# Moving the decays of a chunked scan on VectorE, and joining the scan's block to the projection behind it

## Chip, cores, metric

One core of a Trainium2 chip. The metric is the device time of one execution in microseconds; three timed runs of the kernel before gave 2123.28, 2125.17 and 2125.89 (median 2125.17).

## What is computed

Two transformer blocks in a row, on 1024 tokens of width 1024, all in float32: first one with a linear recurrence, attention and an expert layer, then one with a selective state space scan beside a long convolution, an output projection with layer norm, and a gate with another layer norm. The change touches the second block's scan and its output projection. Cut to these (the names are the reference's):

```python
# ssd_chunked: 8 chunks of 128 tokens, 2 groups of 8 heads of width 64, state 128
xdt = xh * dt
a_cs = cumsum(dt * a)                                   # inside each chunk
ldec = exp(where(causal, a_cs[l] - a_cs[s], -inf))
cb = einsum('clgn,csgn->cgls', cc, bc)
y_diag = einsum('cgjls,csgjp->clgjp', cb * ldec, xdt)
states = einsum('clgn,cgjl,clgjp->cgjpn', bc, exp(a_cs[-1] - a_cs), xdt)
h = h * chunk_decay + states                            # from chunk to chunk
y_off = einsum('clgn,cgjpn,cgjl->clgjp', cc, h_before, exp(a_cs))
y = y_diag + y_off + d_skip * xh
y_ssm = group_rms_norm(y * silu(z)) * ssm_norm_g
out = concat([y_ssm, y_conf]) @ w_out + b_out           # 2048 x 1024
h = layer_norm(ALPHA * h + out, ln1_g, ln1_b)
```

`h * chunk_decay` is the decay that the change moves; `... @ w_out` is the projection that it joins to the scan.

## The kernel before

The program is a row of blocks. In a block each engine has its own list of instructions in an order written out by hand, and semaphores order the engines among each other; a block ends for all engines together. Two blocks concern the change.

**The scan's block** (its vector part ends with the scan). The scan runs over 16 steps i = 2c + g: chunk c, head group g. For each step:

- ScalarE: `decays(i)` waits for the cumulated sums, takes eight Relus (L2656), the chunk's decay factor (L2661) and an Exp over 128x1024 (L2664). At the head of a chunk `read_turned(c)` (L2670) copies the turned B matrix out of PSUM, behind `decays` of the even step and ahead of `decays` of the odd one. `conf_high_part` (L2674) is work for the projection.
- GpSimd: one multiply of 128x1024 (L2515), the Exp's result times `cb`. It waits for `cb_ready` of the chunk and for `decay_ready` of the step.
- TensorE: at the end of each odd step `chunk(c + 1)` (L2539 to L2544: eight turns of x, two of B, two products) for the next chunk is issued ahead of that odd step's own `outputs`. `outputs(i)` makes the state's part (L2565), turns the carried part (L2576) and adds the product inside the chunk (L2582). `carried(i + 1)` (L2553) multiplies the state, after `update(i - 1)`.
- VectorE: `carried(i)` (L2853) scales what TensorE's `carried(i)` gave; `evac_y(i - 1)` (L2829, four instructions) takes y out of PSUM; `update(i - 1)` decays the state (L2866, 128x512, all in SBUF) and adds the chunk's part from PSUM (L2867); `chunk_cb` (L2845, odd steps) masks the next `cb`, after `read_turned`; `inputs(i + 1)` (L2819, two instructions) scales the turned x. `chunk(c)` on TensorE waits for `inputs(2c - 1)`, which VectorE issues in the even step 2c - 2.

The state has two halves, one for each head group; `update(i)` touches the half of its own step.

**The projection's block.** `product(s, t, ...)` (L3071) multiplies token tile t with weight unit s in 24 matmuls of 512 columns: for each of eight slices k, high by high, high by low and low by high. The units are split on the chip: ScalarE rounds (`unit_high_part`, L3138) and the rest `ring - high` is taken by VectorE for unit 0 (`first_low`, L3198) and by GpSimd for units 1 to 5 (L3060). The first product of unit 0 waits for the low part slice by slice. `conf_low_part(t)` (L3202) splits the other operand. Then y is gated by z (`gate_y`, L3208; z is loaded by SP at L3025), its squares are summed (`square_sum`, L3213, and `square_sums` on TensorE, L3089), and the residual is loaded and added up from the products (L3253, L3257). The products rotate over seven banks of PSUM, so the eighth product waits for the first addition (`res_part`).

Of the kernel before, what the change touches and what calls it, by code (L numbers as in the profile page):

```python
# [7 lines left out]
F32 = mybir.dt.float32  # L8
F32R = mybir.dt.float32r
U32 = mybir.dt.uint32  # L10
ALU = mybir.AluOpType
# [3 lines left out]
P = 128  # L15
# [37 lines left out]
def program(nc, A, one_hot, out):  # L53
# [55 lines left out]
    with ctx:  # L109
# [2354 lines left out]
        nc.clear_and_free_semaphores(middle_sems)  # L2464
        with nc.Block() as block:
# [33 lines left out]

            @block.gpsimd  # L2500
            def _(pool):
# [7 lines left out]
                for i in range(STEPS):  # L2509
# [5 lines left out]
                    nc.gpsimd.tensor_tensor(by_head, by_head, over_heads, ALU.mult).then_inc(m_ready, 1)  # L2515

            @block.tensor
            def _(pe):
# [107 lines left out]
                for i in range(STEPS):  # L2626
                    if i % 2 and i + 1 < STEPS:
                        chunk(i // 2 + 1)
                    outputs(i)
                    if 2 <= i + 1 < STEPS:  # L2630
                        carried(i + 1)

# [123 lines left out]

            @block.vector
            def _(dve):
# [184 lines left out]
                for i in range(STEPS):  # L2943
# [14 lines left out]


        z_sb = tiles(0, KD)  # L2960
        y_high, y_low = rounded("y_high", 16, [P, KD, S]), rounded("y_low", 24, [P, KD, S])
        z_in = [sem(f"z_in{g}") for g in range(2)]
        gated_y, ysq_ready, ysum_ready, ysum_mm, yroot_ready = (sem(n) for n in (
            "gated_y", "ysq_ready", "ysum_ready", "ysum_mm", "yroot_ready"))
        y_high_ready, y_low_ready, y_scaled = sem("y_high_ready"), sem("y_low_ready"), sem("y_scaled")

        y_rs = rsm[:, 0:2 * NT]

        res = tiles(0, NT)
        h1T_high, h1T_low = rounded("h1T_high", 16, [P, KD, S]), rounded("h1T_low", 24, [P, KD, S])  # L2970
        unit_high = [rounded("unit_high", 34, [P, KD, HALF])[:], ring_low[:, (U_OUT2 + 2) % NU]]
        b_out, ln1_g, ln1_b = tiles(32), tiles(33), tiles(32)

        ple_at = [tiles(8, 12, HALF)[:, (NT * n + t) % 12] for n in range(2) for t in range(NT)]

        bn2 = router_w[:].rearrange("p k e -> p (k e)")[:, 0:12 * NT].rearrange("p (t s) -> p t s", t=NT)
        ln2_g, ln2_b = tiles(14), tiles(15)
        gate_sb = [tiles(32), tiles(33)]  # L2980
        res_in = [sem(f"res_in{j}") for j in range(2)]
        rows_in, tail_in = sem("rows_in"), sem("tail_in")
        ple_in = [sem(f"ple_in{j}") for j in range(3)]
        res_scaled, ln1_b_in = sem("res_scaled"), sem("ln1_b_in")
        unit_high_ready, unit_low_ready = sem("unit_high_ready"), sem("unit_low_ready")
        first_low_ready = sem("first_low_ready")
        out2_mm, res_part = sem("out2_mm"), sem("res_part")
        var1, root1, h1_ready, h1_tr = sem("var1"), sem("root1"), sem("h1_ready"), sem("h1_tr")
        h1T_high_ready, h1T_low_ready = sem("h1T_high_ready"), sem("h1T_low_ready")
        gate_mm, gate_ready, ple_read = (sem(n) for n in ("gate_mm", "gate_ready", "ple_read"))  # L2990

        GATE_LAG = 2
# [341 lines left out]
```

## Time and profile before

| | us |
|---|---|
| median of three runs | 2125.17 |
| profiled execution | 2123.88 |
| its span | 2122.2 |
| TensorE matmul, busy | 2038.4 (96%) |
| VectorE, busy | 1672.5 (79%) |
| ScalarE, busy | 1081.6 (51%) |
| GpSimd, busy | 237.5 (11%) |

The span runs from the first to the last instruction of the profiled execution; 1.7 us of that execution lie outside it. The scan takes the span's stretch from about 1753 to 1831 and the projection begins at 1833.8. Times of single instructions are given as start and duration from the span's start. Busy shares over the span don't tell what ends a stage: in the scan all of the engines wait for one another.

### The profile page before, as it was taken

The numbers are of one execution on the slowest core, as the hardware profiler recorded it, in microseconds if no ns is written. First come the engines' busy times: TensorE is split into PE (matmuls) and PEld (weight loads), VectorE is DVE, ScalarE is ACT, GpSimd is POOL, SyncE is SP. The second block draws the span as 40 slices with busy tenths as digits, with TensorE's granted clock in tenths as the row PEclk, the third lists the DMA queues.
The fourth block names the chain that finished last, engine by engine and source line by source line (L and its number), as shares of the span: only waits on it lengthen the run. The fifth ranks groups of instructions, "written<-read, shape, count | busy, mean of one in ns | idle before, by whom it ended". The sixth has DMA issues, their size and how long they took to land. (4 is left out here: it accounts for less than half of the span.)

```text
span 2122.2 us, 25232 instructions
## 1 busy us (share of the span) xinstructions
PE 2038.4 (96%) x9940; PEld 1588.7 (75%) x9940; DVE 1672.5 (79%) x1726; ACT 1081.6 (51%) x1267; POOL 237.5 (11%) x172
## 2 busy tenths in 40 slices
PE   6999999999988999999999989999999998899998
PEld 4767766777736888888888657888888875688876
DVE  5575448875587999999999769999999978955776
ACT  4388418883236777777777542112232168523134
POOL 0200100000000111111110230000000014233040
PEclk9999999999999999999999999999999999999999
DMA  7311332104399999999999631112122245333121
GB/s 296 111 40 40 126 118 75 41 10 102 160 355 346 371 402 393 394 399 390 403 391 398 205 145 43 60 61 79 40 90 99 100 141 197 149 129 119 40 80 60
DMA packets 131495, 381.95 MB, mean 180 GB/s; under 512 B 9735, under 2 KB 22567, under 8 KB 131400
## 3 DMA queue, kind: packets, MB, share of 16 engines
q1 hardware_dynamic: 117640, 341.02, 42.3%
q0 software_dynamic: 7536, 22.70, 4.4%
q10 hardware_dynamic: 6224, 16.93, 2.0%
q8 instruction: 64, 1.05, 0.2%
q14 instruction: 31, 0.25, 0.0%
HBM read 337.49 MB, written 43.07 MB: 179 GB/s over the span
## 5 line engine op out<-in xcount | busy, mean ns | idle before, releaser
L2765 DVE SCALAR_TENSOR_TENSOR arena<-arena,vecs 128x1023 f32<-128x1023 f32 (+14 forms) x240 | 304.3, 1268 | 7.1
L2292 DVE TENSOR_TENSOR w_low<-W,w_high 128x2048 fp32r<-128x2048 f32 x96 | 216.9, 2286 | 33.2 <-ACT w_high L2189 33.2
L2292 DVE TENSOR_TENSOR w_low<-arena,w_high 128x2048 fp32r<-128x2048 f32 x96 | 218.4, 2289 | 19.4 <-ACT w_high L2189 19.4
L2005 PE MATMUL Q<-hT_high,w_high 128*128 128x512 f32 (+1 forms) x736 | 230.3, 392 | 2.6 <-DVE hT_low L2275 1.9
L2005 PE MATMUL Q<-hT_low,w_high 128*128 128x512 f32 (+1 forms) x720 | 225.3, 391 | 0.0
L2189 ACT ACTIVATE w_high<-arena 128x2048 fp32r<-128x2048 f32 x96 | 184.2, 1920 | 73.4 <-PE Q L2080 73.4
L2005 PE MATMUL Q<-hT_high,ring_low 128*128 128x512 f32 x704 | 220.3, 390 | 0.0
L2189 ACT ACTIVATE w_high<-W 128x2048 fp32r<-128x2048 f32 x96 | 184.0, 1919 | 65.9 <-PE Q L2080 63.7
L2018 ACT ACTIVATE w_high<-W 128x1024 fp32r<-128x1024 f32 x44 | 46.6, 1058 | 251.8 <-PE Q L2005 243.0
L2005 PEld LDWEIGHTS Q<-hT_high,w_high 128*128 128x128 f32 (+1 forms) x736 | 135.5, 184 | 35.3 <-DVE hT_low L2275 2.1
L2080 PE MATMUL Q<-w_high,x_high 128*128 128x512 f32 x512 | 160.5, 395 | 1.0 <-DVE x_low L2300 1.0
L2080 PE MATMUL Q<-w_low,x_high 128*128 128x512 f32 x512 | 158.6, 391 | 0.0
L2080 PE MATMUL Q<-w_high,x_low 128*128 128x512 f32 x512 | 158.5, 391 | 0.0
L2005 PEld LDWEIGHTS Q<-hT_low,w_high 128*128 128x128 f32 (+1 forms) x720 | 134.2, 186 | 29.8
L2005 PEld LDWEIGHTS Q<-hT_high,ring_low 128*128 128x128 f32 x704 | 132.7, 188 | 27.7
L2080 PEld LDWEIGHTS Q<-w_low,x_high 128*128 128x128 f32 x512 | 96.8, 189 | 20.4
L2080 PEld LDWEIGHTS Q<-w_high,x_low 128*128 128x128 f32 x512 | 96.7, 189 | 20.3
L2080 PEld LDWEIGHTS Q<-w_high,x_high 128*128 128x128 f32 x512 | 95.7, 190 | 20.1 <-DVE x_low L2300 1.2
L582 PE MATMUL Q<-h_high,in_high 128*128 128x512 f32 x254 | 101.1, 398 | 0.0
L583 PE MATMUL Q<-h_high,ring_low 128*128 128x512 f32 x254 | 99.6, 392 | 0.0
L584 PE MATMUL Q<-h_low,in_high 128*128 128x512 f32 x254 | 99.4, 391 | 0.0
L2428 POOL DMA_INDIRECT tokens_acc<-arena,idx x16 | 50.4, 3150 | 343.7 <-DVE arena L2335 330.1
(504 smaller groups left out, 4138.5 us busy)
## 6 DMA issues: line engine op xcount, KB each, us to landing
arena<-in_w_dram SPq DMA_DIRECT2D x48, 2048.0 KB, 12.4
W<-in_w_dram SPq DMA_DIRECT2D x48, 2048.0 KB, 13.5
W<-in_w_mod_dram SPq DMA_DIRECT2D x12, 2048.0 KB, 8.7
W<-in_w_in_dram SPq DMA_DIRECT2D x12, 2048.0 KB, 8.4
W<-in_w_out_dram SPq DMA_DIRECT2D x6, 2048.0 KB, 9.9
spill<-arena ACTq DMA_DIRECT2D x24, 512.0 KB, 2.7
W<-in_w_in_dram SPq DMA_DIRECT2D x8, 1024.0 KB, 8.7
arena<-spill SPq DMA_DIRECT2D x3, 2048.0 KB, 12.6
```

The costliest lines, as they stand in the source:

```text
L582: nc.tensor.matmul(bank, w_high, h_high, start=first, stop=False)
L583: nc.tensor.matmul(bank, w_low, h_high, start=False, stop=False)
L584: return nc.tensor.matmul(bank, w_high, h_low, start=False, stop=last)
L2005: ins = nc.tensor.matmul(Q[rows, 2 * pair_of(n) + half, :], w[:, k], x[:, k, HALF * half:HALF * half + HALF], start=k == 0 and w is high a ...
L2018: nc.scalar.activation(high, src, ACT.Copy).then_inc(split_high, 1)
L2080: ins = nc.tensor.matmul(Q[:, bank + n, :], x[:, kx], w[:, k, HALF * n:HALF * n + HALF], start=kx == 0 and x is high and w is wh, stop=kx ...
L2189: nc.scalar.activation(split_of(r, j)[0][:], chunk_src(r, j), ACT.Copy).then_inc(high_ready, 1)
L2292: nc.vector.tensor_tensor(wl[:], chunk_src(r, j), wh[:].bitcast(F32), ALU.subtract).then_inc(low_v, 1)
L2428: nc.gpsimd.indirect_dma_start(out=tokens_acc, out_offset=bass.IndirectOffsetOnAxis(ap=idx[:, e:e + 1], axis=0), in_=y_e, in_offset=None, ...
L2765: ins = nc.vector.scalar_tensor_tensor(conf[:, i, j:], u[:, 0:S - j], w, conf[:, i, j:], ALU.mult, ALU.add)
```

## The change

Three edits, and one that follows from them. (1) The decay leaves `update`. A new `fade(i)` makes it, and both decays of a chunk are issued in the even step i: `fade(i - 1)` ahead of `update(i - 1)`, and `fade(i)` behind it, ahead of `inputs(i + 1)`. Chunks 1 to 6 have decays, as before. (2) The projection's block is no block of its own any more: each engine's list follows its list of the scan, and on VectorE and SP waits for the scan's last `outputs` stand where the block's end stood. (3) Unit 0 is split while the scan ends: ScalarE rounds its slices behind its last `conf_high_part`, with waits (`FREED_BY`) for the scan's last reads of the memory that the rounded slices take, and GpSimd takes the rest of the slices behind its last multiply; VectorE's `first_low` is gone.

```diff
+        FREED_BY = {0: (chunk_mm, NT), 3: (from_mm, STEPS - 3), 5: (from_mm, STEPS - 2), 6: (turned_ready, NT)}
...
             @block.sync
...
+                sync.wait_ge(stage_out[1], 16 * (len(staged) // 2))
+                sync.wait_ge(y_mm, STEPS)
+                for g in range(2):
+                    sync.dma_start(z_sb[:, 4 * g:4 * g + 4], spill[20 + 4 * g:24 + 4 * g].rearrange("m p n -> p m n"))\
+                        .then_inc(z_in[g], 16)
...
             @block.gpsimd
...
+                for s in range(6):
...
-                for s in range(1, 6):
...
+                        if t == 0:
+                            pe.wait_ge(unit_low_ready, KD * s + k + 1)
...
-                            pe.wait_ge(*((unit_low_ready, KD * (s - 1) + k + 1) if s else (first_low_ready, k + 1)))
...
+                    for k in range(KD):
+                        if s == 0 and k in FREED_BY:
+                            act.wait_ge(*FREED_BY[k])
+                        nc.scalar.activation(unit_high[s % 2][:, k], ring[slot][:, k], ACT.Copy)\
+                            .then_inc(unit_high_ready, 1)
...
             @block.vector
...
+                def fade(i):
+
+                    c, g = divmod(i, 2)
+                    if 1 <= c < NT - 1:
+                        dve.wait_ge(from_mm, i - 1)
+                        dve.wait_ge(factor_ready, i + 1)
+                        s3 = state[:, HALF * g:HALF * g + HALF].rearrange("p (h n) -> p h n", h=HPG)
+                        v_link(nc.vector.tensor_tensor(s3, s3, decay_of(i).broadcast_to((P, HPG, DK)), ALU.mult))
+
                 def update(i):
...
                         if c:
-                            dve.wait_ge(factor_ready, i + 1)
-                            s3 = sg.rearrange("p (h n) -> p h n", h=HPG)
-                            v_link(nc.vector.tensor_tensor(s3, s3, decay_of(i).broadcast_to((P, HPG, DK)), ALU.mult))
                             ins = nc.vector.tensor_tensor(sg, sg, Q[:, STATE_BANKS[i % 2], :], ALU.add)
...
                         evac_y(i - 1)
+                        if i % 2 == 0:
+                            fade(i - 1)
                         update(i - 1)
+                        if i % 2 == 0:
+                            fade(i)
...
                 conf_low_part(0)
                 evac_y(STEPS - 1)
...
-                for k in range(4):
-                    first_low(k)
                 conf_low_part(1)
-                for k in range(4, KD):
-                    first_low(k)
                 conf_low_part(2)
+                dve.wait_ge(y_out, STEPS)
                 for b in range(4):
                     gate_y(b)
```

The rest of the diff carries the projection's lists over unchanged.

## Rows read from the trace of the kernel before

**Rows 1.** Chain that ended last, by time: start us, us, engine, tile, line.

```profile
1832.98 0.70 DVE ring_low L3198
1833.82 34.56 PE Q L3071 x144
1872.05 55.93 PE Q L3071 x240
```

**Rows 2.** Windows: stretch, us, busy PE PEld DVE ACT POOL, PEclk, DMA, GB/s.

```profile
1771.82:1782.59 10.77, 8.74 (x62) 5.38 (x62) 10.01 (x20) 9.83 (x26) 4.82 (x3) 1.00 0.33 119
1782.59:1794.74 12.15, 10.40 (x62) 6.88 (x62) 9.72 (x20) 8.17 (x22) 4.74 (x2) 0.86 0.27 91
1805.51:1816.29 10.78, 8.75 (x63) 5.39 (x63) 10.02 (x20) 8.18 (x22) 4.69 (x2) 1.00 0.07 25
1830.86:1833.82 2.96, 0.00 (x0) 0.03 (x1) 1.96 (x6) 1.50 (x3) 0.00 (x0) 0.50 0.23 19
1833.82:1841.02 7.20, 7.20 (x25) 5.79 (x25) 6.41 (x10) 2.77 (x6) 0.00 (x0) 0.75 0.98 373
```

**Rows 3.** Timeline of VectorE, one chunk: start us, us, line, op, tiles, [idle].

```profile
1807.00 0.69 DVE L2866 TENSOR_TENSOR arena<-arena,small 128x512 f32<-128x512 f32 x1
1808.44 0.42 DVE L2845 TENSOR_TENSOR W<-Q,tri 128x256 f32<-128x256 f32 x1
1810.68 0.69 DVE L2853 TENSOR_TENSOR W<-Q,W 128x512 f32<-128x512 f32 x1 [0.62 <-PE Q L2553]
1812.32 1.86 DVE L2866 TENSOR_TENSOR arena<-arena,small 128x512 f32<-128x512 f32 x1
1814.94 1.29 DVE L2819 TENSOR_TENSOR arena<-Q,keep 128x512 f32<-128x512 f32 x2
```

**Rows 4.** Timeline of TensorE, same chunk: chunk and the even step's carried.

```profile
1805.51 1.09 PE L2539 MATMUL Q<-ident,arena 128*128 128x128 f32 x8 [0.20 <-DVE W L2819]
1814.96 1.12 PE L2553 MATMUL Q<-arena 128*128 128x512 f32 x2 [1.83 <-DVE arena L2867]
```

**Rows 5.** Timelines of ScalarE and GpSimd, the same chunk.

```profile
1807.31 0.39 ACT L2670 ACTIVATE W<-Q 128x256 f32<-128x256 f32 x1 [2.59 <-PE Q L2544]
1810.06 1.06 ACT L2664 ACTIVATE arena<-arena 128x1024 f32<-128x1024 f32 x1
1811.27 2.37 POOL L2515 TENSOR_TENSOR arena<-arena,W 128x1024 f32<-128x1024 f32 x1
```

**Rows 6.** Timelines of TensorE, VectorE and GpSimd, the chunk from 1762.28.

```profile
1762.28 1.04 PE L2539 MATMUL Q<-ident,arena 128*128 128x128 f32 x8
1760.67 1.29 DVE L2819 TENSOR_TENSOR W<-Q,keep 128x512 f32<-128x512 f32 x2
1769.04 0.68 DVE L2866 TENSOR_TENSOR arena<-arena,small 128x512 f32<-128x512 f32 x1
1769.24 2.70 POOL L2515 TENSOR_TENSOR W<-W 128x1024 f32<-128x1024 f32 x1 [0.56 <-ACT W L2664]
```

**Rows 7.** Timelines of several engines, from the scan's last chunk on.

```profile
1819.72 4.69 POOL L2515 TENSOR_TENSOR W<-W 128x1024 f32<-128x1024 f32 x2 [6.08 <-DVE W L2845]
1854.64 16.88 POOL L3060 TENSOR_TENSOR ring_low<-W,ring_low 128x512 fp32r<-128x512 f32 x8 [30.23 <-ACT ring_low L3138]
1942.03 10.04 POOL L3060 TENSOR_TENSOR ring_low<-W,ring_low 128x512 fp32r<-128x512 f32 x8 [21.30 <-ACT ring_low L3138]
1832.32 4.27 ACT L3138 ACTIVATE unit_high<-W 128x512 fp32r<-128x512 f32 x8 [9.49 <-PEq L2465]
1832.30 0.92 SPq L3025 DMA_DIRECT2D arena<-spill  x2
1840.95 4.63 DVE L3208 TENSOR_TENSOR arena<-arena 128x1024 f32<-128x1024 f32 x4 [0.79 <-DMA arena<-spill]
1877.63 0.69 DVE L3257 TENSOR_TENSOR arena<-arena,Q 128x512 f32<-128x512 f32 x1
1878.86 0.39 PE L3071 MATMUL Q<-unit_high,conf_high 128*128 128x512 f32 x1
```

More of the change, by code:

```diff
@@ L2631, in _, with product @@
                         carried(i + 1)
+                def product(s, t, bank, high, low, first=0, end=KD):
+                    w_high, w_low = unit_high[s % 2], ring_low[:, home_of(U_OUT2 + s)]
+                    for k in range(first, end):
+                        if t == 0:
+                            pe.wait_ge(unit_low_ready, KD * s + k + 1)
+                        for x, w in ((high, w_high), (high, w_low), (low, w_high)):
+                            ins = nc.tensor.matmul(Q[:, bank, :], x[:, k, tile_cols(t)], w[:, k],
+                                                   start=k == first and x is high and w is w_high,
+                                                   stop=k == end - 1 and x is low)
+                    return ins
@@ new lines, in turn_h1, with square_sums @@
+                def turn_h1(t):
+                    pe.wait_ge(h1_ready, t + 1)
+                    if t >= 2:
+                        pe.wait_ge(h1T_low_ready, t - 1)
+                    for k in range(KD):
+                        ins = nc.tensor.transpose(Q[:, 2 * (t % 2) + k // 4, P * (k % 4):P * (k % 4) + P],
+                                                  res[:, t, P * k:P * k + P], ident[:])
+                    ins.then_inc(h1_tr, 1)
+                def square_sums():
+                    pe.wait_ge(ysum_ready, 2)
+                    for g in range(2):
+                        for t in range(NT):
+                            ins = nc.tensor.matmul(Q[:, 7, NT * g + t:NT * g + t + 1], z_sb[:, 4 * g + 3, tile_cols(t)],
+                                                   ones[:, 0:1], start=True, stop=True)
+                    ins.then_inc(ysum_mm, 1)
@@ new lines, in _ @@
+                for s in range(2):
+                    for t in range(NT):
+                        i = NT * s + t
+                        if s == 0:
+                            pe.wait_ge(conf_low_ready, t + 1)
+                        if i in Y_BANKS:
+                            pe.wait_ge(y_out, STEPS - 2 + Y_BANKS.index(i) + 1)
+                        if i >= CONF_BANKS:
+                            pe.wait_ge(res_part, i - CONF_BANKS + 1)
+                        product(s, t, i % CONF_BANKS, conf_high, conf_low).then_inc(out2_mm, 1)
+                        if i == 5:
+                            square_sums()
@@ new lines, in _ @@
+                for i, (s, t) in enumerate(y_order):
+                    if s == 2:
+                        pe.wait_ge(y_low_ready, t + 1)
+                    for g in range(2):
+                        j = 2 * i + g
+                        pe.wait_ge(res_part, LEAVE if j < 4 else LEAVE + j - 3)
+                        product(s, t, 4 + j % 4, y_high, y_low, 4 * g, 4 * g + 4).then_inc(out2_mm, 1)
+                    if s == 3 and t in TURNS:
+                        turn_h1(TURNS[t])
+                for i, (n, t) in enumerate(g_order):
+                    if i < 4:
+                        pe.wait_ge(res_part, PARTS - 3 + i)
+                    else:
+                        pe.wait_ge(gate_ready, i - 3)
+                    if n == 0:
+                        pe.wait_ge(h1T_low_ready, t + 1)
+                    product(4 + n, t, 4 + i % 4, h1T_high, h1T_low).then_inc(gate_mm, 1)
+                    if i < len(LATE):
+                        turn_h1(LATE[i])
@@ L2969, in program @@
[L2969 to L2988, printed above, removed]
```

313 lines of the change are left out of this document (124 added, 189 removed).

## The prediction

> **What bounds the kernel now.** I read the chain of waits first, from its end. From 1833.82 on it is TensorE almost alone: the chain enters the output projection through one ScalarE rounding and one VectorE subtraction of the first weight unit and then stays on L3071 [rows 1]. So what lies ahead of 1833.82 moves the end of the kernel one for one, unless something behind it is late in its turn. The table by stage comes second: a chunk of the scan lasts 10.77 us from one start of `chunk` on TensorE to the next, 12.15 in the one with the clock at half speed for a part, and between the scan's last matmul and the first one of the projection TensorE does nothing for 2.96 us [rows 2]. Third, one chunk on each engine. I count from the start of `chunk` on TensorE, 1805.51; that start waited for VectorE's `inputs` [rows 4].
>
> The chunk is a ring of two halves. TensorE runs `chunk`, the odd step's `outputs` and `carried` without a pause; VectorE waits 0.62 us for that `carried` and goes on at 1810.68, 5.17 in [rows 3]. Then VectorE works alone: `carried`, `evac_y`, a decay, an add, `inputs`, and the next `chunk` may start. In this half the decay (L2866) takes 1.86 us instead of 0.69. It began at 1812.32 and ended at 1814.18; GpSimd's second multiply ran from 1811.27 to 1813.64 [rows 3, 5]. The decay ended 0.54 after it, and where GpSimd is idle it takes 0.69: it stood behind GpSimd. The other decay, at 1807.00, lies in the first half, where VectorE has 0.62 us over [rows 3].
>
> **Both decays in the even step.** No instruction is added or removed; six decays change place (i = 2, 4, ... 12), from the half where VectorE has time into the half where everybody waits for it. Each costs 0.72 us there: a decay and an add took 1.44 from 1807.00 to `chunk_cb` at 1808.44 [rows 3], and the add is as long as the decay. What could pay for it is GpSimd: without the decay, `chunk_cb` comes earlier, GpSimd may start its two multiplies earlier, and the blocked decay is released earlier. `chunk_cb` also needs ScalarE's `read_turned`, which ended at 1807.70, so it moves from 1808.44 to some 1807.8, by 0.6 [rows 3, 5]. The first multiply follows. But the second one also needs ScalarE's Exp of the same step, 1810.06 to 1811.12, and it started at 1811.27, 0.15 later: it can hardly start sooner [rows 5]. ScalarE's work hangs on `read_turned`, so on the start of the chunk, and doesn't move in the ring. So the first decay still ends at 1814.18, the add follows, the second decay adds its 0.72, and the ring grows by 0.70 (0.02 given back, bounds 0.1 if the second multiply followed `chunk_cb` in full, and 0.72). Four chunks run in this state, from 1771.82 to 1816.29: +2.8 us.
>
> The first two chunks are different, since ScalarE is the late one there. At i = 2 the decay pushes `inputs` from 1760.67 to 1761.39, it ends near 1762.7, and the `chunk` that began at 1762.28 begins 0.47 later [rows 6]. The next even step is the dear one. Its first decay ran at 1769.04, 0.20 ahead of GpSimd's multiply at 1769.24, which had to wait for it (2.70 us against 2.37) [rows 5, 6]. 0.47 later it would come at 1769.51 and finds GpSimd at work until 1769.24 + 2.37 = 1771.61. It ends at 1772.17; then the add (0.72), the second decay (0.72), `inputs` with its 1.35 to the next `chunk` (1814.94 to 1816.29) [rows 2, 3]: 1774.99 instead of 1771.82, +3.17. Were it early enough to slip in, the second decay would be the blocked one, and +2.2 would be left. The last chunk has no second decay and costs nothing. Scan: 3.17 + 4 x 0.70 = +6.0 us, bounds 2.5 and 6.0, and I take the upper one, since the Exp is the nearest row.
>
> That holds one slow chunk, as before had one: 12.15 against 10.77 us, 1.38, when the granted clock fell to the lower of its levels after TensorE had stood still for 1.8 us before a `carried` (as at 1814.96) [rows 2, 4]. After the change the same pause is followed by a second one, of 0.9 us ahead of `chunk` instead of 0.2. So a fall is at least as likely in each chunk: none gives -1.4, two +1.4, three +2.8.
>
> **One block, first unit split at the scan's end.** ScalarE's eight roundings (L3138) and the subtractions move behind the scan's last multiply, and VectorE's eight subtractions L3198 (0.70 us each, [rows 1]) go to GpSimd, beside the scan's last steps. In before's own times, as if the scan hadn't moved: GpSimd is through with the scan at 1819.72 + 4.69 = 1824.41 [rows 7]. Its eight subtractions take 10.04 us when VectorE is at other things and 16.88 when VectorE subtracts all the while, 1.25 and 2.11 each [rows 7]. Beside VectorE's last decay and three `conf_low` parts I put down 0.55 + 8 x 1.25 + 3 x 0.86 = 13.1, so the last part is there at 1837.5; the ends are 1834.5 and 1841.3. ScalarE stood idle for 9.49 us there [rows 7], and its roundings wait at most for the scan's last `carried`, so they aren't late.
>
> The Trainium skill, "GPSIMD Engine Reference", section 4.1 Engine selection, says that GpSimd is about two times slower than VectorE on elementwise work with two inputs, which speaks against this move. The rows give 1.25 against 0.70, 1.8 times [rows 1, 7]; by the rule (1.40 each, an estimate) the last part would come 1.2 us later, TensorE would gain 1.6 instead of the 1.8 below, and the sum would be +4.4 instead of +4.2.
>
> TensorE then goes from the scan straight into the first product, at 1830.86 instead of 1833.82. Before, that product took 7.20 us, with the clock at half speed for its first part [rows 2]; the same from 1830.86 ends at 1838.1, and GpSimd's last part allows 1838.2. Against 1841.02 that is 2.8 us. But the gain isn't kept. The eighth product, at 1878.86, must not overwrite its bank before VectorE has added the first product to the residual, which before was done at 1877.63 + 0.69 = 1878.32 [rows 7]. VectorE gets there through the loads of z (issued at 1832.30, waited for until 1840.95), the gating, the square sums and the loads of the residual [rows 7]. The z loads are now issued when the last `outputs` is done, at some 1830.95, 1.35 earlier, and all of that chain moves by 1.35: the first add is done at 1876.97, and TensorE gains 1878.86 - 1877.02 = 1.8 us. Removing `first_low` from VectorE, some 5 us, brings nothing more: it waited for z behind them. Bounds: a loss of 1.0, if the last part comes at 1841.3 and its three matmuls, 0.7, follow it, and a gain of 2.9. Moved with the z loads on SP are the two row loads and unit 1; SP had nothing else to send. The new wait for `y_out` on VectorE stands behind its own `evac_y` and costs nothing.
>
> **Sum.** +6.0 - 1.8 = +4.2 us. The profiled execution took 2123.88 (span 2122.2), 1.29 under the median of 2125.17: it would take 2128.1, and the median 2129.4. About 0.2% (4.25 us) is what a measurement of this kernel can tell from no change, so the forecast lies on that edge.
>
> **Rivals.**
> *The falls of the clock multiply.* For it: the longer second pause. Two falls 2130.8, three 2132.2. Against: of the four steady chunks only one was slow.
> *The joint pays for the scan, so not slower.* The place is the first product. If GpSimd and VectorE don't hold each other up there and the residual is early, TensorE gains the whole pause, 2.96, and the half-speed part, about 1.6 us (7.20 against the 5.6 of an undisturbed product, 55.93 us for ten, [rows 1, 2]): -4.5. With +4.6 in the scan (no slow chunk) that is 2125.2. It decides from the point where the eighth part is ready by 1836. Against it: 2.11 us each beside VectorE, and the residual's 0.54 us of slack.
> *The second multiply does follow `chunk_cb`.* Then the ring grows by 0.1, the scan costs 3.17 + 0.4 = +3.6, without a slow chunk +2.2, and with the joint's best -4.5 the time is 2122.9; to be faster by over 0.2% the early loss must be absent too: 2120. Against it: the multiply that starts 0.15 behind the Exp.
>
> **How the numbers follow.** Forecast 0.55 (by the bounds of the joint, 2128.3 to 2132.2); more falls 0.27; joint pays 0.12; multiply follows 0.06, of which faster by over 0.2% 0.03. Slower by over 0.2% (over 2129.4): half the forecast and nearly all of the falls, 0.52; same 0.45; faster 0.03. Range: 2125.0 to 2132.5 takes in two falls, most of the third, and the case in which the joint pays; outside are 0.1 below and 0.08 above.
>
> **What would show it.** Steady chunks of 11.5 us with two decays in each even step, 1.86 and 0.69; a first decay near 1769.5 that is stretched; the Exp still 0.15 ahead of the second multiply; no pause between the scan and the first product, and its last weight part near 7 us behind the scan's last matmul; a wait for the residual ahead of the eighth product. Wrong it is if chunks stay near 10.8, or if the first product runs without waiting for GpSimd.

## The result and the profile after

| | before | after |
|---|---|---|
| median of 11 runs each, us | 2124.80 | 2130.27 |
| profiled execution | 2123.88 | 2131.65 |
| its span | 2122.2 | 2129.9 |
| VectorE busy | 1672.5 | 1670.8 |
| GpSimd busy | 237.5 | 250.5 |

The ratio is 1.0027, with a 95% interval of 1.0016 to 1.0038: slower by 5.5 us, against a forecast of 2129.4 and +4.2. The profiled execution of after is 1.4 us above its median and that of before 0.9 below, so the two traces differ by 7.8 us. One execution of *half multiply* (below) took 7246 us; it stands in that kernel's median and not in its ratio. Below, the joint is short for edits (2) and (3), the joined block with its first unit split early. The two traces can be lined up by the start of the same work (us from the span's start; the last matmul of the scan and the square sums are read as the start or the end of their rows on TensorE):

| | before | after | difference |
|---|---|---|---|
| chunk 1 starts | 1753.05 | 1752.86 | -0.19 |
| chunk 2 | 1762.28 | 1762.53 | +0.25 |
| chunk 3 | 1771.82 | 1774.76 | +2.94 |
| chunk 4 | 1782.59 | 1787.74 | +5.15 |
| chunk 5 | 1794.74 | 1799.23 | +4.49 |
| chunk 6 | 1805.51 | 1812.07 | +6.56 |
| chunk 7 | 1816.29 | 1824.88 | +8.59 |
| the scan's last matmul ends | 1830.86 | 1839.42 | +8.56 |
| square sums start | 1868.22 | 1874.40 | +6.18 |
| eighth product starts | 1878.86 | 1886.68 | +7.82 |

The scan loses 8.6 us, the first products win 2.4 back, and 1.6 of these are lost again behind the square sums. The rows for each, in the columns of the rows of before:

Stretches of after: three chunks of the scan (chunks 2, 3 and 4), then the first product of the projection. They answer to [rows 2].

```profile
1762.53:1774.76 12.23, 8.79 (x63) 5.39 (x63) 10.74 (x20) 10.72 (x30) 5.57 (x3) 1.00 0.77 278
1774.76:1787.74 12.98, 10.38 (x62) 6.98 (x62) 9.86 (x20) 8.18 (x22) 4.74 (x2) 0.87 0.27 83
1787.74:1799.23 11.49, 8.74 (x62) 5.40 (x63) 10.01 (x20) 8.18 (x22) 4.73 (x2) 0.97 0.25 96
1839.49:1846.87 7.38, 5.91 (x23) 4.24 (x24) 4.47 (x6) 0.00 (x0) 6.83 (x4) 0.99 0.86 302
```

The second chunk lasts 12.23 us (9.54 before, from 1762.28 to 1771.82); a chunk that no fall of the clock lengthens 11.49, where it was 10.77 (its mean clock of 0.97 comes from a fall at its end, while TensorE waits); one with the lower level for a part 12.98, with a mean clock of 0.87. Three of the four chunks from 1774.76 on are of that kind (12.98, 12.84, 12.81), before it was one. The first product shows the reverse: 1.00 but for a hundredth instead of 0.75, with TensorE busy for 5.91 of 7.38 us.

VectorE in after, the even step of chunk 4, which started at 1787.74; the answer to [rows 3].

```profile
1790.05 0.42 DVE L3065 TENSOR_TENSOR W<-Q,tri 128x256 f32<-128x256 f32 x1
1792.92 0.69 DVE L3073 TENSOR_TENSOR W<-Q,W 128x512 f32<-128x512 f32 x1 [1.25 <-PE Q L2653]
1794.56 1.85 DVE L3084 TENSOR_TENSOR arena<-arena,small 128x512 f32<-128x512 f32 x1
1796.44 0.69 DVE L3093 TENSOR_TENSOR arena<-arena,Q 128x512 f32<-128x512 f32 x1
1797.16 0.69 DVE L3084 TENSOR_TENSOR arena<-arena,small 128x512 f32<-128x512 f32 x1
1797.89 1.29 DVE L3039 TENSOR_TENSOR W<-Q,keep 128x512 f32<-128x512 f32 x2
```

Two decays (L3084) with the add (L3093) between them: 1.85 and 0.69. The wait for `carried` ahead of them has grown from 0.62 to 1.25: this is the half that lost a decay and had time over anyway.

TensorE in the same chunk, `carried` and the next `chunk`; the answer to [rows 4].

```profile
1797.18 1.12 PE L2653 MATMUL Q<-arena 128*128 128x512 f32 x2 [1.82 <-DVE arena L3093]
1799.23 1.12 PE L2639 MATMUL Q<-ident,arena 128*128 128x128 f32 x4 [0.92 <-DVE W L3039]
```

The pause ahead of `carried` is the old one (1.82; before 1.83), that ahead of `chunk` went from 0.20 to 0.92.

ScalarE's Exp and GpSimd's second multiply of the same chunk; the answer to [rows 5].

```profile
1792.28 1.06 ACT L2826 ACTIVATE W<-W 128x1024 f32<-128x1024 f32 x1
1793.48 2.37 POOL L2608 TENSOR_TENSOR W<-W 128x1024 f32<-128x1024 f32 x1 [0.57 <-ACT W L2826]
```

The Exp ends at 1793.34 and the multiply starts at 1793.48, 0.14 later. It ends at 1795.85 and the blocked decay at 1796.41, 0.56 later.

GpSimd and VectorE in the chunk from 1762.53; the answer to [rows 6].

```profile
1769.03 2.36 POOL L2608 TENSOR_TENSOR W<-W 128x1024 f32<-128x1024 f32 x1 [0.57 <-ACT W L2826]
1769.34 2.59 DVE L3084 TENSOR_TENSOR arena<-arena,small 128x512 f32<-128x512 f32 x1
```

GpSimd comes first now, by 0.31 us; before, VectorE did, by 0.20. The decay takes 2.59 us instead of 0.68 and ends 0.54 after the multiply.

From the scan's end on: GpSimd's low parts of the first unit, SP's loads of z, TensorE's two longest waits for low parts, VectorE's first gating and first residual addition, the eighth product. The answer to [rows 7].

```profile
1832.96 13.36 POOL L2615 TENSOR_TENSOR ring_low<-W,unit_high 128x512 fp32r<-128x512 f32 x8
1839.51 0.92 SPq L2565 DMA_DIRECT2D arena<-spill  x2
1845.13 0.50 PE L2740 MATMUL Q<-unit_high,conf_high 128*128 128x512 f32 x1 [1.21 <-POOL ring_low L2615]
1846.37 0.50 PE L2740 MATMUL Q<-unit_high,conf_high 128*128 128x512 f32 x1 [0.26 <-POOL ring_low L2615]
1847.41 4.63 DVE L3201 TENSOR_TENSOR arena<-arena 128x1024 f32<-128x1024 f32 x4 [3.45 <-DMA arena<-spill]
1883.14 0.69 DVE L3247 TENSOR_TENSOR arena<-arena,Q 128x512 f32<-128x512 f32 x1
1886.68 0.39 PE L2740 MATMUL Q<-unit_high,conf_high 128*128 128x512 f32 x1
```

The last low part ends at 1846.32, 6.9 us behind the scan's last matmul, and the loads of z leave 0.1 us behind it. The eighth product starts without a wait: the residual's first addition was done at 1883.83, 2.85 us ahead of it.

The chain that ended last (start, us, engine, tile, line); the answer to [rows 1].

```profile
1832.99 13.34 POOL ring_low L2615 x8
1846.37 28.19 PE Q L2740 x123
1878.71 57.09 PE Q L2740 x240
```

The way into the projection no longer leads over ScalarE and VectorE but over GpSimd's eight subtractions. In the scan ahead of them the chain stands, chunk after chunk, on `chunk` (L2639), `carried`, `evac_y`, the first decay (L3084), the add, the second decay and `inputs`, so both decays are on the path, as the prediction had them.

### The profile page after: what moved, and what is told of

Its sections match the earlier page's. It is cut to its first block and busy times, and to the rows that moved or that the text cites. A ratio compares the mean times of both kernels' runs of the same rounds, so it can differ in the third digit from the quotient of the medians.

```text
span 2129.9 us, 25231 instructions
## 1 busy us (share of the span) xinstructions
PE 2042.3 (96%) x9940; PEld 1592.0 (75%) x9940; DVE 1670.8 (78%) x1718; ACT 1081.7 (51%) x1267; POOL 250.5 (12%) x180
## 3 DMA queue, kind: packets, MB, share of 16 engines
q8 instruction: 64, 1.05, 0.2%
```

## The experiments

The theory was the prediction's: the scan pays, because both decays stand in the half of the ring where all wait for VectorE; GpSimd's second multiply holds the first of them, and is itself held by ScalarE's Exp; more low clock on top; the joint brings little. Rivals: the joint costs the time (GpSimd's slow low parts), the low clock alone does, the blocked decay alone does. First, all kernels in one table. The profile of each is of one execution, whose time stands in the table: that of *joint only* and that of *odd step, short* are the fastest of their kernels, those of *odd step* and *split squares* the slowest. Ahead of the scan, where these kernels are alike, the profiles differ too: chunk 0, TensorE's first work of the scan, starts between 1731.2 us (*odd step, short*) and 1739.0 (before). So sums over whole profiles hold only roughly, and times of stages are compared inside the stage. Ratios are against runs of before on the same chip (their medians are 2125.05 for the first four, 2123.88 for the next four, 2123.91 for the last two).

| kernel | median us | profiled us | ratio, 95% interval | chunk that no fall lengthens |
|---|---|---|---|---|
| joint only | 2124.07 | 2119.36 | 0.9998, 0.9988 to 1.0008 | 10.77 |
| decays only | 2131.80 | 2131.80 | 1.0036, 1.0022 to 1.0050 | 11.48 |
| both decays in the odd step | 2114.53 | 2118.59 | 0.9951, 0.9938 to 0.9964 | 9.50 |
| Exp ahead | 2125.07 | 2125.65 | 1.0000, 0.9992 to 1.0009 | 10.88 |
| half multiply | 2120.06 | 2119.59 | 0.9983, 0.9973 to 0.9992 | 10.40 |
| odd step, short | 2111.83 | 2104.19 | 0.9949, 0.9934 to 0.9964 | 8.88 |
| low parts on VectorE | 2130.85 | 2130.74 | 1.0034, 1.0021 to 1.0047 | 11.50 |
| filled pause | 2127.72 | 2126.64 | 1.0013, 1.0004 to 1.0023 | 11.49 |
| split squares | 2127.77 | 2134.04 | 1.0017, 1.0007 to 1.0027 | 11.49 |
| odd step, short, split squares | 2110.04 | 2109.28 | 0.9935, 0.9921 to 0.9949 | 8.88 |

### Joint only

After, with each decay back in its own step.

```diff
-                        if i % 2 == 0:
-                            fade(i - 1)
+                        fade(i - 1)
                         update(i - 1)
-                        if i % 2 == 0:
-                            fade(i)
```

> The changed kernel with each decay back in its own step; block and first unit stay joined. Theory (the joint gains about 1.8 us, held by the residual's chain, and the moved decays alone cost the rest): about 2123, 0.1% faster than before, steady chunks of 10.8 us with one stretched decay of 1.86. Rival (the joint gains the whole pause and the half-speed part, 4.5): 2120.5. Rival (the joint itself costs, since GpSimd feeds the first product): 2126 or more.

Measured: 2124.07 us, not to be told from before. One chunk of the scan, then the scan's last `carried`, `conf_low`, the first matmul of the projection and the square sums:

```profile
1780.88:1791.65 10.77, 8.74 (x62) 5.38 (x62) 10.01 (x20) 8.18 (x22) 4.69 (x2) 1.00 0.29 99
...
1823.69 1.13 PE L2653 MATMUL Q<-arena 128*128 128x512 f32 x2 [1.64 <-DVE arena L3093]
1826.51 2.31 DVE L3055 TENSOR_TENSOR conf_low<-arena,conf_high 128x1024 fp32r<-128x1024 f32 x1
1828.87 0.50 PE L2740 MATMUL Q<-unit_high,conf_high 128*128 128x512 f32 x1 [1.40 <-DVE conf_low L3055]
1863.69 3.63 PE L2758 MATMUL Q<-ones,arena 128*128 128x1 f32 x32
```

The same two ends of that stretch in before:

```profile
1825.74 1.12 PE L2553 MATMUL Q<-arena 128*128 128x512 f32 x2 [1.68 <-DVE arena L2867]
1868.22 3.83 PE L3089 MATMUL Q<-ones,arena 128*128 128x1 f32 x32
```

The chunk is the old one, 10.77. So the joint does not cost the time: what after loses comes from the decays. What it wins, the medians can't tell: 0.98 less, with an interval from 2.6 less to 1.7 more. In the traces the stretch from the start of the scan's last `carried` to the square sums tells it: 42.48 us in before (1825.74 to 1868.22) and in *decays only*, 40.00 here (1823.69 to 1863.69), 40.09 in after, 39.96 to 40.09 with the Exp ahead, the half multiply, the filled pause and the split squares. So the joint wins 2.4 to 2.5 us in front of the square sums. Two long waits are left in it: the first matmul waits 1.40 us for `conf_low`, which takes VectorE 2.31 us beside GpSimd's subtractions (1826.51 to 1828.82) instead of the 1.22 that it takes alone, and a later one 1.14 us for GpSimd's low parts.

### Decays only

Before, with the decays moved and the two blocks as they were.

```diff
                         evac_y(i - 1)
+                        if i % 2 == 0:
+                            fade(i - 1)
                         update(i - 1)
+                        if i % 2 == 0:
+                            fade(i)
```

> The kernel before with only the decays moved; VectorE still splits the first unit in a block of its own. Theory: +6 us with as many slow chunks as before, +7.4 to +8.8 with one or two more: 2131 to 2134, steady chunks of 11.5 us, the first stretched decay (i = 4) of 2.6 and the chunk from 1762 of 12.2. Rival (the joint is what costs): no change, 2125.

Measured: 2131.80 us, 6.75 above before and in the range expected (2131 to 2134). Two chunks of it:

```profile
1774.12:1787.10 12.98, 10.84 (x64) 7.08 (x63) 9.55 (x20) 8.18 (x22) 4.74 (x2) 0.83 0.26 90
1787.10:1798.58 11.48, 8.74 (x62) 5.39 (x62) 9.99 (x20) 8.18 (x22) 4.74 (x2) 1.00 0.27 93
```

These are the chunks of after, 12.98 and 11.48. With the joint's -0.98 the two halves add up to +5.8, and the whole change measures +5.5.

### Both decays in the odd step

The mirror of the change: after, with both decays in the odd step, ahead of its add.

```diff
-                        if i % 2 == 0:
+                        if i % 2:
                             fade(i - 1)
+                            fade(i)
                         update(i - 1)
-                        if i % 2 == 0:
-                            fade(i)
```

> The changed kernel with both decays in the odd step, ahead of the add, instead of the even one: the same instructions, moved the other way. Theory (in the odd step VectorE has time over, and there GpSimd isn't multiplying, so the decay isn't stretched): VectorE's lone half of the ring loses the stretched 1.86 and ends 5.2 + 3.7 into the chunk; chunk_cb comes 0.7 later and with it GpSimd's first multiply, which then holds the even step's outputs. Chunks of about 9.3 to 9.6 us, 1.2 to 1.5 less than before, about 2116 to 2118. Rival (the place of the decays doesn't matter, all VectorE work of a chunk is paid): 2123 to 2125 as with the joint alone. Rival (a later chunk_cb costs more than the stretch saves): over 2125.

Measured: 2114.53 us, 0.49% below before. A chunk, and in it VectorE's decays and GpSimd's multiplies:

```profile
1782.67:1792.17 9.50, 8.85 (x63) 5.39 (x62) 8.83 (x19) 8.19 (x23) 4.70 (x2) 1.00 0.30 111
...
1784.51 1.41 DVE L3084 TENSOR_TENSOR arena<-arena,small 128x512 f32<-128x512 f32 x2
1787.18 4.70 POOL L2608 TENSOR_TENSOR W<-W 128x1024 f32<-128x1024 f32 x2 [4.80 <-DVE W L3065]
```

The same twelve decays, on the same engine: 1.41 us for a pair, none of them stretched, since they are over at 1785.92 and GpSimd starts at 1787.18. A chunk takes 9.50 us, 1.27 below before and 1.99 below after. The chunk came out as expected (9.3 to 9.6), the time 1.5 us under the expected 2116. The mean clock is 1.00 in chunks 2 to 6. What counts is which half of the ring the decays lie in.

### ScalarE's Exp ahead

After, with `read_turned` behind the odd step's `decays` instead of ahead of it from chunk 3 on. It takes away what holds GpSimd's second multiply.

```diff
-                    if g == 0:
+                    if g == (c >= 3):
                         read_turned(c)
```

> The changed kernel, with ScalarE's odd decays put ahead of read_turned from chunk 3 on, into the time in which ScalarE is idle. Theory (the second multiply starts when that Exp is done): the Exp is now done before the chunk begins, the second multiply follows the first at 5.1 to 5.2 behind the chunk's start instead of 5.74, ends 0.6 earlier, and the stretched decay with it: chunks of 10.9 instead of 11.5, about 2.5 to 3 us under the changed kernel, 2127 to 2128. Rival (the second multiply already starts when GpSimd is free, or the decay is slow for another reason): chunks stay at 11.5, 2130.

Measured: 2125.07 us. GpSimd's multiplies and VectorE's first decay in a chunk of 10.88 us:

```profile
1790.18 4.70 POOL L2608 TENSOR_TENSOR W<-W 128x1024 f32<-128x1024 f32 x2 [6.18 <-DVE W L3065]
1794.18 1.25 DVE L3084 TENSOR_TENSOR arena<-arena,small 128x512 f32<-128x512 f32 x1
```

The second multiply now follows the first without a wait (two in 4.70 us), and the first decay takes 1.25 instead of 1.85. The chunk is 0.61 shorter than in after, 0.60 of it from that decay: 10.9 was expected. The time is 1.9 us under the expected 2127; in the profile one chunk of the four from chunk 3 on is lengthened by the clock, in after three. So the Exp did hold the multiply, and through it the decay; and the two moved decays still cost 0.1 per chunk against before.

### Half of the second multiply

After, with GpSimd multiplying only four of the eight heads in odd steps from chunk 3 on; the other four are left unmultiplied.

```diff
+                    if g and c >= 3:
+                        by_head, over_heads = by_head[:, 0:4], over_heads[:, 0:4]
                     nc.gpsimd.tensor_tensor(by_head, by_head, over_heads, ALU.mult)...
```

> The changed kernel; from chunk 3 on GpSimd multiplies only four of the eight heads in the odd steps (the other four are left without the mask and the product, so part of the scan's result is left out). It measures by itself whether the stretched decay is stretched by GpSimd. Theory: the second multiply starts at 5.74 behind the chunk's start as before, lasts 1.2 instead of 2.37 and ends near 6.95; the decay that comes at 6.8 then takes 0.8 instead of 1.85, and chunks from 3 on last 10.4 instead of 11.5: about 2126, or less if the clock falls less often. Rival (the decay is slow for another reason, such as the wait for the factor): it stays at 1.85 and the chunks at 11.5, 2130.

Measured: 2120.06 us. GpSimd's halved multiply and VectorE's two decays in a chunk of 10.40 us:

```profile
1788.46 1.28 POOL L2610 TENSOR_TENSOR W<-W 128x512 f32<-128x512 f32 x1 [0.57 <-ACT W L2828]
1789.53 0.76 DVE L3086 TENSOR_TENSOR arena<-arena,small 128x512 f32<-128x512 f32 x1
1791.05 0.69 DVE L3086 TENSOR_TENSOR arena<-arena,small 128x512 f32<-128x512 f32 x1
```

The multiply starts 0.14 behind the Exp as in after and ends at 1789.74; the decay beside it takes 0.76 and ends at 1790.29, 0.55 later. 1.09 us taken from GpSimd gave 1.09 to the decay (1.85 to 0.76) and to the chunk (11.49 to 10.40). With that the blocked decay is shown to be on the ring in full. The chunk came out as expected, 10.40, the time did not: 2120 instead of 2126. In the profile one chunk from chunk 3 on, of 11.99, has the lower clock, where after has three, and the stay at the lower clock behind the square sums is the shorter one (below): 2 x 1.4 + 1.6 = 4.4 us less. That would account for most of the 6 if the other executions were like the profiled ones, which no run shows.

### Odd step, short

The mirror, with `evac_y` behind `inputs` in every step, to see how far that idea goes.

```diff
+                    if i % 2:
+                        fade(i - 1)
+                        fade(i)
                     if i:
-                        evac_y(i - 1)
-                        if i % 2 == 0:
-                            fade(i - 1)
                         update(i - 1)
-                        if i % 2 == 0:
-                            fade(i)
...
                         inputs(i + 1)
+                    if i:
+                        evac_y(i - 1)
```

> Both decays in the odd step, as the run with the odd step, and evac_y moved behind inputs in every step, so that chunk_cb and GpSimd's first multiply start 1.0 earlier. Theory (there the first multiply, 0.5 late, holds the even step's outputs, and the ring is what counts): GpSimd is in time, the ring is TensorE's own work, and VectorE is busy all the time: chunks of 9.0 to 9.1 instead of 9.5, 2112 to 2113 against 2114.5. Rival (evac_y's new place holds outputs, which wait for it): 9.5 or longer, 2115 or more.

Measured: 2111.83 us. A chunk; then GpSimd's low parts of the first unit and the last of TensorE's waits for them:

```profile
1782.25:1791.13 8.88, 8.48 (x64) 5.47 (x63) 8.74 (x21) 8.21 (x24) 4.71 (x2) 1.00 0.34 121
...
1808.13 13.86 POOL L2615 TENSOR_TENSOR ring_low<-W,unit_high 128x512 fp32r<-128x512 f32 x8
1822.05 0.51 PE L2740 MATMUL Q<-unit_high,conf_high 128*128 128x512 f32 x1 [1.24 <-POOL ring_low L2615]
```

A chunk takes 8.88 us (9.0 to 9.1 expected), of which VectorE is busy 8.74: the scan is now bound by VectorE. Chunks 3 to 6 are 0.62 shorter each than with both decays in the odd step, 2.5 us in all, but the ratio is the same within the intervals. Part of it the joint takes back: from the start of the scan's last `carried` to the square sums it is 41.96 us here (1808.08 to 1850.04), 1.9 more than the 40.0 to 40.1 of the even-step kernels above (41.28 with both decays in the odd step, where that `carried` itself ran at the lower clock, 2.08 us instead of 1.12). The low parts end at 1821.99, 10.1 us behind the scan (6.9 in after): a shorter scan leaves GpSimd less time beside it. The rest isn't shown: six executions of this kernel spread from 2104 to 2118 us.

### The first unit's low parts on VectorE

After, with the eight subtractions on VectorE behind the last `evac_y`; the block stays joined.

```diff
-                for s in range(6):
+                for s in range(1, 6):
...
+                for k in range(4):
+                    first_low(k)
                 conf_low_part(1)
+                for k in range(4, KD):
+                    first_low(k)
                 conf_low_part(2)
```

> The changed kernel, joined block and all, but VectorE takes the first unit's low parts, as before the change, behind its last evac_y. If GpSimd's pace is what the first product waits for (theory: its last part is there 6.9 us behind the scan's last matmul), VectorE's parts at 0.7 each come 1.7 to 6.8 us behind it, no later, and the first product waits for the first part instead: it starts 1.8 later and ends at about the same time; 2130, same as the changed kernel. Rival (the exchange of turns with GpSimd costs VectorE's chain to z and the residual): faster, 2128. Rival (VectorE's eight parts delay the gating): slower, 2131 to 2132.

Measured: 2130.85 us, the same as after, as expected. The first matmul of the projection:

```profile
1839.92 0.47 PE L2741 MATMUL Q<-unit_high,conf_high 128*128 128x512 f32 x1 [1.92 <-DVE ring_low L3227]
```

It starts 1.92 us behind the scan and TensorE then waits once more, for 0.48 us, while after starts at once and waits for GpSimd. To the square sums it is 35.41 us from the scan's end here, 34.98 in after and 37.37 in before. That the subtractions moved to the slower engine is no cause of the loss, and no help either.

### A filled pause

After, with one more matmul, whose result is overwritten, ahead of the even step's `carried` (i = 5, 7, ... 13), so that TensorE stands still for a shorter time.

```diff
-                    pe.wait_ge(state_ready, i - 1)
...
+                    if g and 5 <= i < STEPS - 1:
+                        nc.tensor.matmul(Q[:, FROM_BANK, :], bc_conv[...], bc_conv[...], start=True, stop=True)
+                    pe.wait_ge(state_ready, i - 1)
```

> The changed kernel with one matmul more on TensorE, whose result is overwritten, ahead of the even step's carried, in the pause of 1.8 us (from i = 4 to 12). It measures what the falls of the clock cost. Theory (the clock falls behind these pauses, and a fall on a chunk costs 1.3 to 1.4): the extra matmul of about 1 us delays nothing, chunks all last 11.5 us, three slow chunks fewer than in the profiled run of the changed kernel: about 2127 to 2128. Rival (the falls have nothing to do with the pause): 12.8 as often as before, 2130.

Measured: 2127.72 us. Two chunks, and `carried` behind the filled pause:

```profile
1797.40:1808.88 11.48, 9.80 (x65) 5.69 (x65) 10.00 (x20) 8.18 (x22) 4.72 (x2) 1.00 0.28 93
1808.88:1821.49 12.61, 11.46 (x65) 7.00 (x65) 9.46 (x20) 8.18 (x22) 4.73 (x2) 0.86 0.01 5
...
1795.35 1.13 PE L2656 MATMUL Q<-arena 128*128 128x512 f32 x2 [0.76 <-DVE arena L3096]
```

The pause of 1.82 is down to 0.76. From chunk 2 on four chunks take 11.48 or 11.49 us, one 12.61 at a clock of 0.86; after had three slow ones. The ratio, 1.0013, lies 0.0014 (3 us) below after's 1.0027, and the two intervals overlap (1.0004 to 1.0023 and 1.0016 to 1.0038). That fits the account in which the pauses bring the low clock, and doesn't prove it: one profile each, and one fall is still there. The other profiles add to it. Of chunks 3 to 6, the clock lengthens 10 of 16 in the four kernels with pauses of about 1.8 and 0.9 us (after, decays only, low parts on VectorE, split squares), 3 of 12 where the first pause is 0.7 to 1.2 (Exp ahead, half multiply, filled pause), 3 of 8 with 1.8 and 0.2 (before, joint only), and none of 12 in the three odd-step kernels, whose pauses are 0.4 to 0.5.

### Split squares, alone and with the short odd step

After, with the square sums (32 one-column matmul records in the trace, from 16 matmuls in the code) in two halves, behind products 6 and 7; then the same on the kernel *odd step, short*.

```diff
-                        if i == 5:
-                            square_sums()
+                        if 5 <= i < 7:
+                            square_sums(i - 5)
```

> The changed kernel, with the projection's 32 one-column matmuls of the square sums issued in two halves, behind the sixth and the seventh product, instead of all behind the sixth. It asks where the joint's gain goes behind the first products. Theory (TensorE's clock falls behind that stretch of 3.7 to 4.2 us, for one step or two at 1.6 us each, and nothing waits for the residual): the stretch from the square sums to the first product with y is 59.0 to 60.6 instead of 60.6 to 62.2, the time 1 to 3 us under the changed kernel, 2127.5 to 2129. Rival (the eighth product waits for the residual, as was forecast): TensorE stands still ahead of it and nothing is gained, 2130.

> Both decays in the odd step and evac_y behind inputs, with the square sums in two halves as well: the best that the runs point to. Theory: chunks of 8.9 us as before, and 0 to 2 us off behind the square sums: 2110 to 2112 against 2111.8. Rival (the halves cost what they save): 2112.

Measured: 2127.77 us and 2110.04 us. In the first, the eighth product:

```profile
1885.68 0.47 PE L2740 MATMUL Q<-unit_high,conf_high 128*128 128x512 f32 x1 [0.24 <-DVE arena L3248]
```

Here the residual is late, by 0.24 us, 44.3 us behind the scan's end (1841.34). The stretch from the square sums to the first product with y takes 61.01 us (59.0 to 60.6 expected, 62.23 in after): the fall of the clock now comes behind the second half. A further fall later on takes that gain back, and from the square sums to the span's end it is 255.98 us here and 255.53 in after. In the second kernel the stretch to the first product with y takes 59.08, as without the split (59.02). Neither gain is outside the intervals: 1.0017 (1.0007 to 1.0027) beside after's 1.0027, and 0.9935 (0.9921 to 0.9949) beside 0.9949. So the traces show no gain from split squares, and whether they help is left open. The second kernel is the fastest of all, 13.9 us below before on the same chip.

## Why the prediction was right, and where it was not

**The scan, a steady chunk: right.** Forecast 11.5 with decays of 1.86 and 0.69 and the Exp 0.15 ahead of the multiply; measured 11.49, 1.85, 0.69 and 0.14. That `chunk_cb` comes 0.6 earlier and the first multiply with it, and that it helps nobody, is also as forecast: `chunk_cb` starts 2.31 behind the chunk's start (2.93 before), and the first multiply leaves GpSimd idle for 0.57 before the second. Undoing the move gave 10.77 back; removing the Exp's hold gave 10.88, halving the multiply 10.40. The rival *second multiply follows `chunk_cb`* gave +0.1 per chunk as its price, and that is what the kernel with the Exp ahead shows: the price was right, the condition is not there in after.

**The dear second chunk: right, in this execution.** First decay forecast near 1769.5, blocked for 2.6; measured 1769.34 and 2.59. The next chunk was put at 1774.99 and came at 1774.76, and *decays only* shows the same (12.21 us). But it hangs on which engine comes first at i = 2: in the profiles of the Exp ahead, the half multiply, low parts on VectorE, the filled pause and the split squares chunk 1 is the dear one instead, with 12.1 to 12.5 us (9.67 in after), part of it from a lower clock (0.76 to 0.86), and chunk 2 takes 11.5 to 12.0. There the decay of that step finds the multiply at work and takes 1.18 to 2.35 us; in after it came 0.50 us ahead of the multiply and took 0.69.

**The low clock: undersized.** The forecast kept one slow chunk, the profile of after has three. By the sum of the prediction, +6.0 + 2 x 1.4 = +8.8 for the scan; measured +8.56. So the rival *the falls multiply* happened, in this execution with its three chunks. It had 0.27, and the forecast's own reasoning, a second pause of 0.9 us in each chunk, speaks for more than that; in one chunk of four in before, with one pause, the clock had fallen, and in the kernels with both pauses it lengthened 10 chunks of 16. The medians (+5.5) stand between one slow chunk (+4.2) and two (+5.6).

**The joint, first product: right in size.** GpSimd's last part was put near 7 us behind the scan, with 13.1 for it all; measured 6.9 and 13.36, 1.67 each, between the 1.25 and the 2.11 of [rows 7] (2.11 was measured beside VectorE's squares and `conf_low` parts, not beside subtractions alone). The first products win 2.39 us (37.37 to 34.98 from the scan's end to the square sums, with the scan's last `outputs` at the lower clock in both), forecast 2.8. What the forecast had no term for is `conf_low`: VectorE's 1.22 us became 2.31 beside GpSimd, and in after it was done at 1839.44, 0.05 us ahead of the first product, in an execution in which the scan's last product inside the chunk took 1.97 us at the lower clock. In the five profiles where that took 1.09 (joint only, Exp ahead, half multiply and both of *odd step, short*) the first product waited 1.18 to 1.41 us for `conf_low`.

**The joint, the residual: wrong.** This is the step that failed: "all of that chain moves by 1.35", so that the eighth product would wait for the residual and TensorE keep 1.8. The eighth product waits for nothing in after. The chain of the residual moved by 3.05, measured from the scan's end: 47.46 before (1878.32 - 1830.86), 44.41 after (1883.83 - 1839.42). Of these 1.35 are the earlier issue, as forecast; 0.75 are loads that land faster (8.65 us from the issue to the first gating before, 7.90 after); and 0.95 come with VectorE's first squares, which took 4.71 in before and 3.74 in after. First before, then after, with GpSimd's subtractions of the second unit:

```profile
1852.31 4.71 DVE L3213 TENSOR_TENSOR arena<-arena 128x1024 f32<-128x1024 f32 x3
...
1858.79 3.74 DVE L3206 TENSOR_TENSOR arena<-arena 128x1024 f32<-128x1024 f32 x3
1861.71 16.56 POOL L2615 TENSOR_TENSOR ring_low<-W,ring_low 128x512 fp32r<-128x512 f32 x8 [15.39 <-ACT ring_low L2933]
```

GpSimd begins 2.92 us into the squares in after and 2.33 in before (1854.64, [rows 7]): counted from the scan's end the squares moved by 2.1 and GpSimd's work only by 1.5. The prediction moved the chain as a rigid piece and forgot that GpSimd's work beside it moves by another amount. That this work is what lengthened the squares is argued from the overlap; no run takes it away. The kernel with split squares shows that the limit exists, 44.3 behind the scan's end; without other losses it would cap the gain at 3.7 us, not at 1.8.

**What took its place.** From the square sums on the granted clock falls, and for longer than before. The stretch from the start of the 32 square sums to that of the eighth product holds these 32 records and the 24 matmuls of one product (the columns of [rows 2]). First before:

```profile
1868.22:1878.87 10.65, 10.65 (x58) 9.35 (x57) 4.64 (x4) 0.27 (x1) 3.30 (x2) 0.84 0.94 379
```

The same stretch of after:

```profile
1874.40:1886.68 12.28, 12.28 (x57) 10.61 (x56) 6.25 (x6) 0.27 (x1) 3.87 (x3) 0.72 0.79 309
```

And of *odd step, short*:

```profile
1850.04:1859.12 9.08, 9.08 (x58) 8.08 (x57) 3.21 (x5) 0.28 (x1) 1.25 (x1) 1.00 0.87 348
```

9.08 us at a clock of 1.00, 10.65 at 0.84 and 12.28 at 0.72: a longer stay at the lower level costs 1.6 each time. After lost 1.63 there against before, and 2.39 - 1.63 = 0.76 was left of the joint. *Joint only*, with 0.84 there, lost nothing behind the squares, so that in its profile the whole 2.5 of its first products was left, more than the forecast's 1.8. What decides whether the stay is the shorter or the longer one is open: of the kernels like after, those with the joint alone, the Exp ahead, the half multiply and the filled pause show the shorter one, and after, the odd step and the low parts on VectorE the longer one, each in one profile; in *odd step, short* the clock didn't fall there at all.

**The sum.** Forecast +6.0 - 1.8 = +4.2; by the traces +8.56 - 0.75 = +7.8; by the medians +5.5. The main term, the decays, was right to 0.2 us: 8.56 less the 2.8 of the two further falls is 5.8, against 6.0. Both misses of the trace, 2.6 in the low clock of the scan and 1.05 in the joint, are mostly TensorE's clock, and they go the same way. That the loss comes out near the forecast is no luck in the scan's decays. It is luck in the joint, where a cap that did not act and a loss that was not foreseen stood for one another; and between the two traces the forecast is off by 3.6 us, between the medians by 1.3.

## What to carry to other kernels

Price a moved instruction by the half of the ring it lands in, not by its length: the same decays cost 0.72 us a chunk in the half that all wait for, and saved 1.27 in the half where their engine had time, and the mirror of a losing move is worth a run. Before you count on a blocked instruction being released earlier, list everything that its blocker waits for (here the multiply waited for the Exp, 0.14 us ahead of it, and freeing it was worth 0.6 a chunk). When work behind a stage moves earlier, move what shares an engine or a memory port with it as well, before you call a wait the next bound.

## What the runs showed of the hardware

In this kernel GpSimd's multiply and a VectorE operation that reads two operands from SBUF (the on-chip memory; PSUM, the matmuls' memory, is apart from it) didn't run side by side: the decay ended 0.54 to 0.56 us behind GpSimd's multiply wherever it started during one, whether that held it up for 1.9 us (2.59 long), for 1.2 (1.85) or hardly at all (0.76, beside the multiply of half the size). `evac_y`, which reads PSUM, wasn't held: its four instructions took 1.11 us during the multiply of 1793.48, as they do elsewhere in after. The Trainium skill, "SBUF — State Buffer", section "SBUF: two separate sides", states that whichever of such a pair starts first holds the shared ports for its whole instruction and the other blocks fully; the trace agrees, in both orders: GpSimd's multiply took 2.70 when the decay was 0.20 ahead of it [rows 6], and 2.36 when it was 0.31 ahead of the decay.

Low clock where TensorE had not paused: with the square sums, 32 one-column records without a gap, the granted clock fell for a shorter or a longer stay in nine of the ten profiles that have them in one piece, and the stretch with the product after them cost 1.6 or 3.2 us more than the 9.08 at a clock of 1.00 in the tenth (*odd step, short*). In the scan a fall cost 1.1 to 1.6 us a chunk (12.61 against 11.49 with the filled pause, 11.99 against 10.40 with half a multiply). In chunks 3 to 6 of the three odd-step kernels (9.50 and 8.88 us), in which TensorE waits little, the clock was 1.00 throughout; in their chunk 1, behind a wait of 2.7 to 5.4 us for a load, it was 0.78 to 0.83.
